# A decoder step on one core: value pages ahead of the last prompt sums, masked values on ScalarE, two roundings of the head outputs, keys transposed ahead of a split

## The chip, the cores and the metric

The kernel runs on one core of one Trainium2 chip. The metric is the device time of one execution in microseconds (us). TensorE (PE) multiplies matrices into PSUM, VectorE (DVE) and ScalarE (ACT) do the element-wise work, GpSimd (POOL) builds constants and issues the small loads and all of the state and cache outputs, and SyncE (SP) issues the large loads.

## What is computed

Two decoder layers, for 256 prompt tokens and for 8 decoding samples of 4 tokens each, 288 columns in all. A layer is a gated feed-forward block (FFN), a mixer, and a second FFN, each between a conditioned normalisation and a gated residual. The mixer runs three kinds of heads side by side and projects their outputs:

```
def mixer(a, w_in, w_out, ...):
    gq, gk, gv, gg, glr, mu, mv, sq, sk, sv = split_cols(a @ w_in)
    o_gla, s_gla = gla_mixer(gq, gk, gv, gg, glr, ..., gla_s0)      # 4 heads, recurrent state
    o_gm, v_gm = gmlp_mixer(mu, mv, ...)                            # 4 heads, spatial gating
    kk, vv = past keys and values (8 pages of 128 per sample), then the new ones
    o_sb = sb_attend(hs(sq), kk, vv, pos0, sb_b)                    # 8 heads, stick-breaking attention
    o = jnp.concatenate([o_gla, o_gm, o_sb], axis=-1) @ w_out
```

In the stick-breaking attention the weight of a key is exp(log_sigmoid(z) + a suffix sum of -softplus(z)). For the prompt this is a chain of matmuls with triangular matrices and element-wise steps for each of four head pairs; for the samples the keys and values come from pages of a cache in HBM.

## The kernel before

Activations lie transposed, features on the 128 partitions and the 288 columns in the free dimension. Every large matrix product is made of three fp32r products: weights and activations are split into a rounded part and a rest, `w_hi`, `w_lo` and `a_hi`, `a_lo`. For a weight step of 256 columns SP loads two halves of 512 KB into `raw` (two slots), ScalarE rounds each half into `w_hi` and VectorE makes `w_lo` (the helper `split`), and TensorE multiplies 48 times (16 output and input block pairs, three products each).

One loop body holds a layer, so each line below runs twice. The order of the work is written out by hand, engine by engine: every engine runs its own list in order and waits on semaphores. What stands behind a waiting instruction on the same engine waits too.

The mixer's input product has twelve weight steps (MI 0 to 11). After steps 3 to 10 TensorE multiplies two chunks of key pages each (`key_chunk`, 16 chunks of 4 pages, 1 MB each, in four slots of `direct`). VectorE transposes each chunk in place first (`turn_keys`, L1750). `KEYS_AT` gives the two chunks of a step. SP has the loads of key chunks 0 to 3 between those of steps 3 and 4. ScalarE's list has, in step 3, first the split of step 5, then the copy of the row bias (L1336), for which TensorE's sum of the means (L885) waits.

Then comes the stretch without weight steps, some 95 us in each layer. TensorE's list there mixes: the prompt pairs' scores, sums (`prompt_sums`, L933 and L934) and values (`prompt_values`, L944 and L946); the recurrent heads; the samples' value pages (`value_chunk(0..15)`, L830, 16 chunks through the same four slots of `direct`: chunk n is loaded once chunk n-4 has been used); `new_values` (L841), which closes a group of four samples; transposes of new key and value rows for the outputs (`rows_of`, L953); and the update of the samples' state, a product of `gvk` with `vm` (L1112), the value rows masked for each sample, which GpSimd makes (L2104) in the memory of slot 0 of `raw`.

When both groups of samples are done, ScalarE copies the sums out (`sample_rows`, L1424), TensorE transposes them (`turn_rows`, L849), ScalarE puts the heads in place in `Y` (`sample_heads`, L1435), and `Y` is rounded in four pairs of blocks, all 288 columns at a time, into `a_hi` (L1487) and `a_lo` (L1988). Then the output product runs its four steps (MO 0 to 3). Its first step is:

```
pe.wait_ge(lo_done.sem, lo_done.at(l, 2 * POS_MO + 2))
pe.wait_ge(yb_free.sem, yb_free.at(l, KB + 2 + 1))
last = paired_products(0, (0, 1), lambda k: pe.wait_ge(heads_ready.sem, heads_ready.at(l, k + 1)))
```

`yb_free` is raised by ScalarE at L1492, behind its split of MO step 1: `split(l, POS_MO, 0, 1)` and then `act.sem_inc(yb_free.sem, 2)`. The arrays `gvk`, `a_turn` and `a_keys` share memory with `w_hi`; `kst`, `o_rows` and `S` share memory with `w_lo`. So the splits of MO steps 0 and 1 wait for `outs_done`, which GpSimd raises when its output DMAs have landed.

## Time and profile before

| | us |
|---|---|
| median of 3 runs | 1523.11 |
| lowest, highest | 1519.5, 1530.31 |
| the profiled execution | 1520.16 |
| its span, first to last instruction | 1518.6 |
| TensorE busy | 1392.4 (92%) |
| VectorE busy | 822.9 (54%) |
| ScalarE busy | 589.5 (39%) |
| GpSimd busy | 56.5 (4%) |

The mean granted TensorE clock is 0.961 of full speed. The two layers repeat the same program: the mixer of the first lies at about 302 to 524 us of the span, that of the second at about 1036 to 1258 us.

### The profile page before, as it was taken

What the parts mean: (1) busy time and instruction counts of PE and PEld (TensorE: products, weight loads), DVE (VectorE), ACT (ScalarE), POOL (GpSimd) and SP (SyncE); (2) the same over time, 40 slices, a digit from 0 to 9 for tenths busy, and PEclk for the clock granted to TensorE, in tenths of its full rate; (3) what the DMA queues carried; (4) which work ended last, traced back from release to release, by engine and by line L of the source; (5) the groups of instructions that cost most, each with busy time, mean ns of one, the idle gap of its engine ahead of it and who ended that gap; (6) DMA issues with size and microseconds to landing.
All of it is one profiled execution on the core that took longest, in us unless ns stands there. A gap on an engine that the chain in (4) does not pass through costs nothing.

```text
span 1518.6 us, 36144 instructions
## 1 busy us (share of the span) xinstructions
PE 1392.4 (92%) x13844; PEld 1301.6 (86%) x13844; DVE 822.9 (54%) x1221; ACT 589.5 (39%) x949; POOL 56.5 (4%) x130
## 2 busy tenths in 40 slices
PE   5899999989886899999979999998997778999996
PEld 4899999789764889999969999987995577999996
DVE  2544544657972564554454455355789336455544
ACT  2423333523533543334453333354253345333344
POOL 3000000100110000000000000010002100000000
PEclk9899999999988999999989999999998979999998
DMA  9797597699757795555658858859994769765453
GB/s 313 244 279 220 158 303 219 189 295 292 243 198 239 238 319 160 163 149 150 181 161 278 256 160 253 261 171 282 273 301 163 254 179 322 209 165 166 142 164 113
DMA packets 432268, 335.16 MB, mean 221 GB/s; under 512 B 16087, under 2 KB 356343, under 8 KB 432128
## 3 DMA queue, kind: packets, MB, share of 16 engines
q1 hardware_dynamic: 429556, 327.52, 70.4%
q0 software_dynamic: 2272, 5.61, 1.1%
q8 instruction: 92, 1.51, 0.4%
q14 instruction: 48, 0.39, 0.1%
q10 hardware_dynamic: 300, 0.13, 0.0%
HBM read 328.41 MB, written 4.78 MB: 219 GB/s over the span
## 4 chain that ended last, share of the span: by engine, by line
PE 76%; DVE 7%; DMA 4%; SPq 4%; ACT 3%; issue 3%; DVEq 2%; ACTq 0%
PE PS L554 19%; PE PS L555 19%; PE PS L556 19%; PE PS L578 3%; PE PS L599 2%; PE PS L600 2%; PE PS L601 2%; PE PS L784 2%; SPq L460 2%; SPq L439 1%; PE PS L723 1%; PE PS L830 1%; PE PS L933 1%; DMA direct<-in_cache_sb_v 1%; DMA raw<-in_mix_w_in 1%
## 5 line engine op out<-in xcount | busy, mean ns | idle before, releaser
L1527 DVE TENSOR_TENSOR w_lo<-raw,w_hi 128x1024 fp32r<-128x1024 f32 (+1 forms) x371 | 396.1, 1106 | 530.7 <-ACT w_hi L1181 530.7
L1181 ACT ACTIVATE w_hi<-raw 128x1024 fp32r<-128x1024 f32 (+1 forms) x371 | 339.8, 960 | 726.1 <-PE PS L556 624.9
L554 PE MATMUL PS<-a_hi,w_hi 128*128 128x288 f32 x1664 | 497.9, 299 | 0.1
L555 PE MATMUL PS<-a_lo,w_hi 128*128 128x288 f32 x1664 | 490.9, 295 | 0.0
L556 PE MATMUL PS<-a_hi,w_lo 128*128 128x288 f32 x1664 | 489.3, 294 | 0.0
L554 PEld LDWEIGHTS PS<-a_hi,w_hi 128*128 128x128 f32 x1664 | 312.0, 188 | 8.2 <-issue 7.5
L556 PEld LDWEIGHTS PS<-a_hi,w_lo 128*128 128x128 f32 x1664 | 313.4, 188 | 0.0
L555 PEld LDWEIGHTS PS<-a_lo,w_hi 128*128 128x128 f32 x1664 | 312.4, 188 | 0.2
L554 PE MATMUL PS<-h_hi,w_hi 128*128 128x288 f32 x704 | 209.8, 298 | 0.0
L555 PE MATMUL PS<-h_lo,w_hi 128*128 128x288 f32 x704 | 209.1, 297 | 0.0
L556 PE MATMUL PS<-h_hi,w_lo 128*128 128x288 f32 x704 | 208.5, 296 | 0.0
L554 PEld LDWEIGHTS PS<-h_hi,w_hi 128*128 128x128 f32 x704 | 133.4, 189 | 2.2 <-issue 1.6
L555 PEld LDWEIGHTS PS<-h_lo,w_hi 128*128 128x128 f32 x704 | 132.1, 188 | 0.2
L556 PEld LDWEIGHTS PS<-h_hi,w_lo 128*128 128x128 f32 x704 | 132.1, 188 | 0.0
L599 PE MATMUL PS<-a_hi,w_hi 128*128 128x288 f32 x256 | 80.7, 315 | 28.3 <-DVE a_lo L1606 19.0
L578 PE MATMUL PS<-direct,cT 128*32 128x128 f32 x2560 | 87.5, 282 | 16.6 <-DMA direct<-in_cond_w 13.6
L578 PEld LDWEIGHTS PS<-direct,cT 128*32 128x32 f32 x2560 | 68.1, 112 | 31.9 <-issue 15.8
L599 PEld LDWEIGHTS PS<-a_hi,w_hi 128*128 128x128 f32 x256 | 51.2, 200 | 32.9 <-DVE a_lo L1606 18.5
L600 PE MATMUL PS<-a_lo,w_hi 128*128 128x288 f32 x256 | 78.6, 307 | 0.0
L601 PE MATMUL PS<-a_hi,w_lo 128*128 128x288 f32 x256 | 78.3, 306 | 0.0
L1750 DVE STREAM_TRANSPOSE direct<-direct 128x2048 f32<-128x2048 f32 x32 | 72.0, 2287 | 0.0
L830 PE MATMUL PS<-direct,a_keys 128*32 128x128 f32 x1024 | 37.0, 295 | 17.6 <-DMA direct<-in_cache_sb_v 13.0
(302 smaller groups left out, 1235.9 us busy)
## 6 DMA issues: line engine op xcount, KB each, us to landing
raw<-in_ffn_w_in SPq DMA_DIRECT2D x180, 512.0 KB, 4.8
direct<-in_cond_w SPq DMA_DIRECT2D x320, 256.0 KB, 4.9
direct<-in_cache_sb_k SPq DMA_DIRECT2D x128, 256.0 KB, 4.0
direct<-in_cache_sb_v SPq DMA_DIRECT2D x128, 256.0 KB, 3.8
...
raw<-in_mix_w_in SPq DMA_DIRECT2D x48, 512.0 KB, 6.9
...
raw<-in_mix_w_out SPq DMA_DIRECT2D x16, 512.0 KB, 6.0
```

The costliest lines, as they stand in the source:

```text
L460: sp.dma_start(direct[:, n % 4, 512 * t:512 * t + 512], src).then_inc(direct_in[n % 4].sem, 16)
L554: pe.matmul(out, whi, hi, start=begins and i == 0, stop=False)
L555: pe.matmul(out, whi, lo, start=False, stop=False)
L556: last = pe.matmul(out, wlo, hi, start=False, stop=ends and i == n - 1)
L578: last = pe.matmul(PS[32 * g:32 * g + 32, 6 + pair, 0:P], cT[:, 4 * half + kb, :], direct[:, slot, kb * 512 + g * P:kb * 512 + g * P + P], ...
L599: pe.matmul(out, whi, a_hi[:, k, :], start=k == 0, stop=False)
L600: pe.matmul(out, whi, a_lo[:, k, :], start=False, stop=False)
L601: last = pe.matmul(out, wlo, a_hi[:, k, :], start=False, stop=k == KB - 1)
L830: last = pe.matmul(PS[32 * p:32 * p + 32, 4, smp * P:smp * P + P], a_keys[:, 4 * half + t, 32 * p:32 * p + 32], direct[:, n % 4, 512 * t + ...
L1181: act.activation(w_hi[:, s, at_:at_ + n], raw[:, s, at_:at_ + n], ACT.Copy)\
L1527: tt(w_lo[:, s, at_:at_ + n], raw[:, s, at_:at_ + n], w_hi[:, s, at_:at_ + n], ALU.subtract).then_inc(lo_done.sem, 1)
L1750: dve.transpose(direct[:, n % 4, :], direct[:, n % 4, :]).then_inc(k_turned.sem, 1)
```

## The change

1. SP loads MI step 4's weights between key chunks 1 and 2; VectorE transposes key chunk 0 in step 2, ahead of its split of step 4, and no longer in step 3.
2. The prompt's and samples' key rows (`rows_of` with SK) are transposed and copied out at the start of the stretch, through bank 4 of PSUM, and no longer around the last prompt sums.
3. `vm` is made by ScalarE with 16 small activations, in slot 1 of `raw`, and no longer by GpSimd. SP loads MO step 0's weights ahead of value chunk 8 into slot 0, which is free for it, and the other steps behind chunk 15.
4. On TensorE value chunks 9, 10 and 11 come ahead of `prompt_sums(3)`, and both `prompt_values` ahead of chunk 14.
5. On ScalarE MO step 0 is split, and all but the samples' columns of blocks 4 to 7 is rounded, ahead of the last `sample_rows` and `sample_heads`; the 32 remaining columns of those four blocks are rounded by one more instruction on each of ScalarE and VectorE.
6. GpSimd's outputs change order, and the samples' state goes out last, behind `outs_done` and behind the last `new_values`.

```
--- before.py
+++ after.py
-        vm = [tile(f"vm{j}", [NS, B, P], F32, BASE + 4096 * j) for j in range(GP)]
+        vm = [tile(f"vm{j}", [NS, B, P], F32, BASE + 8192 + 4096 * j) for j in range(GP)]
...
-                key_chunks(l, 0, 1, 2, 3)
-                mix_in(4, 5)
+                key_chunks(l, 0, 1)
+                mix_in(4)
+                key_chunks(l, 2, 3)
+                mix_in(5)
...
                 for n in range(NPC):
+                    if n == 8:
+                        mix(l, mix_w_out, POS_MO, 0, 0, 0)
                     page_chunk(l, cache_sb_v, DP_V, 4 * n, n, n)
                 sp.wait_ge(ds_sum.sem, ds_sum.at(l, GP))
                 sp.sem_inc(raw_free.sem, 1)
-                for s in range(2):
-                    mix(l, mix_w_out, POS_MO, s, s, s * 256)
+                mix(l, mix_w_out, POS_MO, 1, 1, 256)
...
+                rows_of(0, SK, 4, k_t)
+                pe.wait_ge(kv_k.sem, kv_k.at(l, 1))
+                rows_of(1, SK, 4, k_t)
                 pe.wait_ge(gla_in.sem, gla_in.at(l, 1))
...
                 turn_new(0)
+                pe.wait_ge(kv_k.sem, kv_k.at(l, 2))
+                rows_of(2, SK, 4, k_t)
...
                 prompt_sums(2, 0)
+                value_chunk(9)
+                value_chunk(10)
+                value_chunk(11)
+                prompt_sums(3, 2)
                 pe.wait_ge(o_std.sem, o_std.at(l, 1))
-                rows_of(0, SK, 6, k_t)
-                rows_of(1, SK, 7, k_t)
-                value_chunk(9)
-                prompt_sums(3, 2)
...
-                value_chunk(10)
-                pe.wait_ge(o_headed.sem, o_headed.at(l, 1))
-                rows_of(2, SK, 5, k_t)
-                value_chunk(11)
                 value_chunk(12)
+                value_chunk(13)
                 pe.wait_ge(c_sub.sem, c_sub.at(l, 3))
                 prompt_values(0, 0)
-                value_chunk(13)
+                pe.wait_ge(c_sub.sem, c_sub.at(l, 4))
+                prompt_values(1, 2)
                 value_chunk(14)
                 value_chunk(15)
                 new_values(1)
-                pe.wait_ge(c_sub.sem, c_sub.at(l, 4))
-                prompt_values(1, 2)
-                pe.wait_ge(kv_k.sem, kv_k.at(l, 3))
+                pe.wait_ge(o_headed.sem, o_headed.at(l, 1))
                 turn_rows(1)
...
-                            heads_ready.sem, heads_ready.at(l, k + 1)))
+                            heads_ready.sem, heads_ready.at(l, k + 1 if k < 2 else KP + 1)))
...
+                def values_by_sample():
+                    for j in range(GP):
+                        for b in range(B):
+                            last = act.activation(vm[j][:, b, :], gvk[0:NS, 2, j * P:j * P + P], ACT.Copy,
+                                                  scale=same_s[:, b:b + 1])
+                        last.then_inc(vm_ready.sem, 1)
...
                 sample_weights(0)
+                key_rows(0, 4)
+                key_rows(1, 4)
                 prompt_scores(2)
...
                 weights_by_page(0)
+                key_rows(2, 4)
                 gla_rows(0, 6)
...
                 prompt_log1p_exp(1)
+                values_by_sample()
                 sample_weights(1)
...
                 act.wait_ge(outs_done.sem, outs_done.at(l, 1))
-                split(l, POS_MO, 0, 0, only=(0,))
-                sample_heads(1)
-                split(l, POS_MO, 0, 0, only=(1,))
-
-                act.drain()
+                act.wait_ge(ds_sum.sem, ds_sum.at(l, GP))
+                split(l, POS_MO, 0, 0)
                 act.wait_ge(gla_done.sem, gla_done.at(l, 1))
                 act.wait_ge(gm_done.sem, gm_done.at(l, 1))
+                act.wait_ge(op_sum.sem, op_sum.at(l, 2))
                 for k in range(KP):
                     if k >= 2:
                         act.wait_ge(op_evac.sem, op_evac.at(l, k - 1))
-                    act.activation(a_hi[:, 2 * k:2 * k + 2, :], Y[:, 2 * k:2 * k + 2, :], ACT.Copy)\
+                    n = T if k < 2 else NP
+                    act.activation(a_hi[:, 2 * k:2 * k + 2, 0:n], Y[:, 2 * k:2 * k + 2, 0:n], ACT.Copy)\
                         .then_inc(heads_round.sem, 1)
+                sample_rows(1)
+                sample_heads(1)
+                act.drain()
+                act.activation(a_hi[:, 4:8, NP:T], Y[:, 4:8, NP:T], ACT.Copy).then_inc(heads_round.sem, 1)
                 split(l, POS_MO, 0, 1)
...
                             .then_inc(q_rep.sem, 1)
+                        turn_keys(0)
...
                     for n in KEYS_AT.get(j, ()):
-                        turn_keys(n)
+                        if n:
+                            turn_keys(n)
```

VectorE in input step 2 and 3: `qrep` is the copy that ends step 2's first part, `w_lo` of 1024 columns a half of a weight split, `direct` a chunk of key pages. Before:

```order
L1805 COPY qrep<-Fm 128x512 [waits mix_evac]
L1526 REGISTER_ALU
L1527 TENSOR_TENSOR w_lo<-raw,w_hi 128x1024 [waits hi_done]
L1526 REGISTER_ALU
L1527 TENSOR_TENSOR w_lo<-raw,w_hi 128x1024 [waits hi_done]
L1809 STREAM_TRANSPOSE qt<-PS 128x512 [waits q_t]
L1744 TENSOR_TENSOR qb<-qt,row_part 128x512
L1749 ISA
L1750 STREAM_TRANSPOSE direct<-direct 128x2048 [waits direct_in0]
L1750 STREAM_TRANSPOSE direct<-direct 128x2048 [waits direct_in1]
```

The same place after the change:

```order
L1818 COPY qrep<-Fm 128x512 [waits mix_evac]
L1762 ISA
L1763 STREAM_TRANSPOSE direct<-direct 128x2048 [waits direct_in0]
L1539 REGISTER_ALU
L1540 TENSOR_TENSOR w_lo<-raw,w_hi 128x1024 [waits hi_done]
L1539 REGISTER_ALU
L1540 TENSOR_TENSOR w_lo<-raw,w_hi 128x1024 [waits hi_done]
L1823 STREAM_TRANSPOSE qt<-PS 128x512 [waits q_t]
L1757 TENSOR_TENSOR qb<-qt,row_part 128x512
L1763 STREAM_TRANSPOSE direct<-direct 128x2048 [waits direct_in1]
```

The transpose of chunk 0 stands ahead of the split of step 4, that of chunk 1 where it was.

ScalarE at the end of the stretch: `o_rows` and `Y` are `sample_rows(1)` and `sample_heads(1)`, `raw_in00` and `raw_in01` the two halves of MO step 0, `raw_in10` and `raw_in11` those of MO step 1. Before:

```order
L1405 ACTIVATE zp<-zp 128x768 [waits c_sub]
L1424 ACTIVATE o_rows<-PS 128x512 [waits o_rows_sum]
L1177 ISA [waits outs_done]
L1181 ACTIVATE w_hi<-raw 128x1024 [waits w_used,raw_in00]
L1435 ACTIVATE Y<-PS 64x4x4 [waits o_turned]
L1435 ACTIVATE Y<-PS 64x4x4 x7
L1181 ACTIVATE w_hi<-raw 128x1024 [waits raw_in01]
L1487 ACTIVATE a_hi<-Y 128x576 [waits gm_done,gla_done]
L1487 ACTIVATE a_hi<-Y 128x576
L1487 ACTIVATE a_hi<-Y 128x576 [waits op_evac] x2
L1181 ACTIVATE w_hi<-raw 128x1024 [waits w_used,raw_in10]
L1181 ACTIVATE w_hi<-raw 128x1024 [waits raw_in11]
```

The same place after:

```order
L1180 ISA [waits ds_sum,outs_done]
L1184 ACTIVATE w_hi<-raw 128x1024 [waits w_used,raw_in00]
L1184 ACTIVATE w_hi<-raw 128x1024 [waits raw_in01]
L1496 ACTIVATE a_hi<-Y 128x576 [waits op_sum,gm_done,gla_done]
L1496 ACTIVATE a_hi<-Y 128x576
L1496 ACTIVATE a_hi<-Y 128x2x256 [waits op_evac] x2
L1434 ACTIVATE o_rows<-PS 128x512 [waits o_rows_sum]
L1445 ACTIVATE Y<-PS 64x4x4 [waits o_turned]
L1445 ACTIVATE Y<-PS 64x4x4 x7
L1501 ACTIVATE a_hi<-Y 128x4x32
L1184 ACTIVATE w_hi<-raw 128x1024 [waits w_used,raw_in10]
L1184 ACTIVATE w_hi<-raw 128x1024 [waits raw_in11]
```

The split of step 0 and four roundings moved ahead of the samples' copies; one small rounding is left behind them, and the split of step 1, behind which `yb_free` is raised, stayed last.

TensorE from value chunk 9 on: `direct` with `a_keys` is a value chunk (16 rows of it stand as one and x15), `zp` with `sv` are `prompt_values`, `sn` with `suffix` the sums of pair 3. Before:

```order
L953 MATMUL PS<-ident,Fm 128x128 [waits o_std]
L953 MATMUL PS<-ident,Fm 128x128 x7
L830 MATMUL PS<-direct,a_keys 32x128 [waits direct_in1]
L830 MATMUL PS<-direct,a_keys 32x128 x15
L933 MATMUL PS<-sn,suffix 128x384 [waits sp_ready]
```

After:

```order
L833 MATMUL PS<-direct,a_keys 32x128 [waits direct_in1]
L833 MATMUL PS<-direct,a_keys 32x128 x15
L833 MATMUL PS<-direct,a_keys 32x128 [waits direct_in2]
L833 MATMUL PS<-direct,a_keys 32x128 x15
L833 MATMUL PS<-direct,a_keys 32x128 [waits direct_in3]
L833 MATMUL PS<-direct,a_keys 32x128 x15
L936 MATMUL PS<-sn,suffix 128x384 [waits sp_ready]
```

The eight key transposes are gone from there, and two more value chunks stand ahead of the sums.

## Rows read from the trace of the kernel before
**Rows 1.** timeline of PE, input steps 3, 4: start, us, line [idle before]
```profile
329.52 1.93 PE L784 MATMUL PS<-direct,qb 128*32 128x128 f32 x32 [4.75 <-DVE direct L1750]
...
335.25 0.64 PE L554 MATMUL PS<-a_hi,w_hi 128*128 128x288 f32 x1
```

**Rows 2.** timeline of ACT in the same place
```profile
323.53 1.06 ACT L1181 ACTIVATE w_hi<-raw 128x1024 fp32r<-128x1024 f32 x1 [0.59 <-DMA raw<-in_mix_w_in]
...
327.34 1.06 ACT L1181 ACTIVATE w_hi<-raw 128x1024 fp32r<-128x1024 f32 x1 [0.34 <-DMA raw<-in_mix_w_in]
328.30 0.15 ACT L1336 ACTIVATE row_bias<-PS 128x1 f32<-128x1 f32 x1
```

**Rows 3.** timeline of SP, the issues of one chunk of pages
```profile
458.29 2.03 SPq L460 DMA_DIRECT2D direct<-in_cache_sb_v  x4
```

**Rows 4.** timeline of POOL in the stretch
```profile
425.10 3.76 POOL L2104 TENSOR_TENSOR vm<-gvk,same_s 32x1024 f32<-32x1024 f32 x2 [11.22 <-ACT gvk L1410]
...
454.09 1.16 POOL L2116 DMA_DIRECT2D out<-sv  x2 [17.79 <-ACT sv L1415]
```

**Rows 5.** timeline of DVE, two instructions for either sample group
```profile
404.14 0.20 DVE L1773 COPY totals<-sm 128x32 f32<-128x32 f32 x1
...
404.32 1.24 DVE L1775 TENSOR_TENSOR z<-z,sm 128x1040 f32<-128x1040 f32 x1
...
425.20 1.83 DVE L1773 COPY totals<-sm 128x32 f32<-128x32 f32 x1
...
427.02 2.94 DVE L1775 TENSOR_TENSOR z<-z,sm 128x1040 f32<-128x1040 f32 x1
```

**Rows 6.** timeline of PE in the middle
```profile
432.50 1.09 PE L1038 MATMUL PS<-wst,vn 128*64 128x128 f32 x16 [2.55 <-DVE att_s L1914]
434.53 0.64 PE L1045 MATMUL PS<-wss,vn 32*64 32x32 f32 x8 [0.93 <-DVE wss L1929]
```

**Rows 7.** stretches: us, busy PE, PEld, DVE, ACT, POOL, clock, DMA, GB/s
```profile
434.50:441.70 7.20, 7.17 (x56) 5.39 (x56) 5.05 (x7) 1.16 (x2) 1.23 (x2) 0.53 0.58 207
...
461.89:478.89 17.00, 12.95 (x238) 8.95 (x236) 4.84 (x6) 4.71 (x7) 3.41 (x5) 1.00 0.66 214
...
496.26:504.25 7.99, 7.99 (x50) 7.99 (x51) 4.13 (x5) 1.79 (x2) 0.00 (x0) 0.81 0.81 220
504.25:510.70 6.45, 6.45 (x51) 6.45 (x50) 2.36 (x2) 3.22 (x5) 0.00 (x0) 1.00 0.42 116
```

**Rows 8.** timeline of ACT at the stretch's start
```profile
416.31 0.62 ACT L1391 ACTIVATE zp<-PS,sb 128x128 f32<-128x128 f32 x2 [3.10 <-DVE zp L1857]
```

**Rows 9.** timeline of PE in the tail
```profile
461.89 1.04 PE L953 MATMUL PS<-ident,Fm 128*128 128x128 f32 x8
...
484.02 1.94 PE L830 MATMUL PS<-direct,a_keys 128*32 128x128 f32 x32 [5.13 <-DMA direct<-in_cache_sb_v]
...
487.75 1.13 PE L944 MATMUL PS<-zp,sv 128*64 128x256 f32 x4
...
490.56 1.12 PE L849 MATMUL PS<-ident,o_rows 128*128 128x128 f32 x4
496.26 0.58 PE L599 MATMUL PS<-a_hi,w_hi 128*128 128x288 f32 x1 [4.58 <-DVE a_lo L1988]
```

**Rows 10.** timeline of ACT in the tail
```profile
462.53 1.09 ACT L1420 ACTIVATE kst<-PS 128x512 f32<-128x512 f32 x2 [2.08 <-PE PS L953]
...
491.71 0.80 ACT L1435 ACTIVATE Y<-PS 64x16 f32<-64x16 f32 x8 [2.29 <-PE PS L849]
```

**Rows 11.** DMA, median us to landing: value chunk 12, MO step 0
```profile
direct<-in_cache_sb_v SPq DMA_DIRECT2D x4, 256.0 KB, 3.8
...
raw<-in_mix_w_out SPq DMA_DIRECT2D x2, 512.0 KB, 8.7
```

**Rows 12.** chain that ended last, 430 to 515 us: chunk 15
```profile
476.25 7.72 DMA direct<-in_cache_sb_v
```

**Rows 13.** list of waits, 300 to 515 us: total, times, longest
```profile
PEld PS L599 <- ACTq L1492: 5.0, 1, 5.0
```

53 lines of the change are left out of this document (24 added, 29 removed).

## The prediction

> **What bounds the kernel now.** TensorE is busy for 1392.4 of 1518.6 us (the table above), so I read where it is not busy, first in the list of waits and then in its timeline with ScalarE's and VectorE's beside it. What this change can reach lies in the two mixers, in six gaps per layer. I work them out in the first layer; the second repeats them. Times are of the profiled execution (1520.16 us), which lies 3.0 us under the median of 1523.11.
>
> **Input steps 3 and 4.** TensorE ends step 3 at about 324.8, then idles 4.75 us until VectorE has transposed key chunk 0 (329.52), and starts step 4 at 335.25 [rows 1]. The chain behind it: the second half of step 4's weights lands at 323.5, the second half of step 5's at 327.3 [rows 2], VectorE splits step 4, turns the queries, and only then transposes two chunks. After the change step 4's weights are asked for two chunks earlier. A chunk's four issues take 2.03 us and a look at the page table before them about 0.6 [rows 3], so the weights land 5.3 us earlier, at 318.2, about when slot 0 of `w_hi` is free again. VectorE transposes chunk 0 while it would idle, has split step 4 by 321, the queries by 322.2 and chunk 1 by 324.5. So TensorE takes chunk 0 at once. From 329.52 to 335.25 the two chunks and the mean take 5.73 us at the lower clock; at the full one half, 2.9. That gives 327.7, but the mean waits for the row bias, which stands in ScalarE's list behind the split of step 5. That weight has the same bytes ahead of it as before, so I take the same landing: bias at 328.4 [rows 2], mean 1.1 us, step 4 at 329.6. **Gain 5.7 us**; 7.5 if step 5's weights land 2 us sooner; 4 if VectorE's chunk 1 slips by 1.5. Behind it the steps are full again: TensorE has some 9 us of work per step, VectorE 7.5, so the shift is kept.
>
> **The middle.** GpSimd makes `vm` from 425.10 for 3.76 us [rows 4]. Just then VectorE's copy of 32 columns takes 1.83 us and its subtraction 2.94; the same two took 0.20 and 1.24 at 404 [rows 5]. With `vm` on ScalarE these 3.3 us go. TensorE waits behind exactly this VectorE chain: 2.55 us at L1038 and 0.93 at L1045 [rows 6], 3.5 us, of which the third key row copy (0.6 on ScalarE, ahead of `gvk`) takes back 0.5: 3.0. Then the clock: from 434.5 to 441.7 TensorE was busy all the time at a granted clock of 0.53, near its lower level of 1.2 GHz [rows 7], right behind these two idle times. About 6.2 of the 7.2 us ran at half speed; at 2.4 GHz they are 3.1, so the clock gives 3.0 if it stays up, 0 if not. Without the two idle times TensorE works on without a break, so I take it. **Gain 6.0**, 2.5 to 6.5.
>
> `vm` itself is 16 activations of 128 columns. The nearest row is a pair of 128 columns with a bias pointer, 0.62 [rows 8], 0.31 each, 5.0 us for 16; the eight of 16 columns in 0.80 [rows 10] bound it below, 1.6. They begin at about 429.9, behind the second prompt exponential, and ScalarE next waits for VectorE's offsets, due near 434; 5.0 us ends at 434.9, and VectorE comes to the result only at about 436.5. So it is hidden; at over 0.4 each it would show.
> The Trainium skill, "ScalarE: Activation LUTs", section "What ACT_TABLE_LOAD costs", gives 186 ns + 0.833 ns per element, 93 ns more for a pointer operand and 93 ns of overlap: an estimate of 0.29 us each here, 4.7 us together; the row's 0.31 is close, and no row shows this form itself.
> The first two key copies stand on ScalarE where it idles 3.10 us for VectorE [rows 8]; with two hops to TensorE they take about 2.6, so the prompt scores behind them start when they did.
> The Trainium skill, "SBUF — State Buffer", section "Who interferes with whom", says that GpSimd and VectorE lock a shared port pair for whole instructions and the later one fully blocks. The trace agrees so far: the slow copy ends where the first half of GpSimd's work does, 427.0. By the rule all 3.3 us go; without it none would, the middle would bring 0, and the time would be 1474.
>
> **The tail.** From 461.89 (key rows, now gone from here) to 478.89 TensorE was busy 12.95 us at full clock [rows 7]: chunks 9 to 14, the last sums, the `vm` product, the first `prompt_values`. Take off the key rows, 1.04 for two and half of it for the third [rows 9]: 11.4. Add chunk 15 and `new_values` (3.73 at the lower clock from 484.02 on, 2.0 at the full one) and the second `prompt_values` (2.81 from 487.75 on, 1.5 at the full one) [rows 9]: 14.9. If nothing is waited for it ends at 476.8. What could be late:
> - The sums of pair 3. ScalarE copied two key rows ahead of the exponential, with 2.08 idle and 1.09 busy [rows 10]; without them its part ends 3.1 us earlier, VectorE's at 464.0, and TensorE arrives at 465.0.
> - Pair 3's weights. TensorE now has chunks 14, 15 and `new_values` queued behind them. Sums end at 466.9, `vm` at 468.8, then VectorE's two state additions and its step to 470.4, ScalarE to 471.3. TensorE arrives at 472.3.
> - Chunk 15. It is asked for when chunk 11 has been used (465.0) and two chunks stand ahead on SP, 2.65 us each: issued by 470.5, landing 3.8 later [rows 11], at 474.3. TensorE arrives at 474.8. Half a microsecond of room, the tightest point.
> - MO step 0's split: its weights landed at 441, the last rows that `outs_done` stands for are asked for at 454 [rows 4] and should land by 462, both before 471.3, when ScalarE is free. Then split (2.0), VectorE's part, and the rounding of four pairs end at 478.6.
>
> From 476.8: `o_rows` copy 0.65, transposes 0.6 (1.12 at the lower clock, [rows 9]), `sample_heads` 0.8 [rows 10], rounding and issue 0.6, in all 479.5; the first step can't start under them, since `yb_free` is raised behind them and behind step 1's split. The list of waits shows that very gate before [rows 13]. It needs step 1's weights, issued at 471, landed by 477 to 479. I take 479.8 against 496.26 [rows 9]: 16.5. MO step 0 ran at 0.81 of the clock for 7.99 us, the next in 6.45 [rows 7]; half of that difference, 0.8. **Gain 17.3**, 12 to 18.
>
> **Sum.** 5.7 + 6.0 + 17.3 = 29.0 a layer, 58 for both: 1520.2 - 58 = 1462. Part of the 3 us to the median added, **1463**. With all lower ends, 4 + 2.5 + 12 = 18.5 a layer, 1483; with the upper ones 32, 1456.
>
> **Rivals.**
> A. *Landings take the gap's place.* The last chunk landed 7.7 us after its issue, and the first output weights 8.7 [rows 11, 12]. If that came again, chunk 15 would land at 477.9, 3.1 late, and step 1's weights, behind it, would hold `yb_free`: 3.5 us a layer, 1470. For it: these very transfers. Against it: then kst and the state went out at the same time, and they no longer do.
> B. *The clock stays low in the middle and falls again before MO*, since shorter idle times ahead of both places remain: 3.8 a layer, 1470.
> C. *The front doesn't do what it says*: step 5's weights or the reordered DMAs land as late as step 4's did, TensorE's wait only moves to the mean: gain 0 to 1, 1472.
> D. *Two or three of these at once*: 1480 to 1492.
> E. *Slower than before*, one mechanism: ScalarE now waits for `outs_done` at 471, ahead of all rounding and of `sample_rows(1)`; before it waited at 488. GpSimd raises it after key, value and prompt state rows have landed. Each us beyond about 474 costs one. The value rows are asked for at 454 [rows 4]; even at the slowest landing above, 8.7, they are there at 464. The stall would have to last 29 us, to 503, for the kernel to lose; it would then give 1523 or more.
>
> **Chances.** Forecast 0.5; A 0.15; B 0.13; C 0.08; D 0.08; nothing gained net 0.03; E 0.03. A measurement of this kernel can tell about 1% (15 us) from no change. All cases but the last two are faster by more: faster 0.94, same 0.03, slower 0.03. The range takes in the forecast with its bounds and A to C, and the lower half of D: 1453 to 1485.
>
> **What would show it.** Step 4 starts some 5 us after step 3's end (10.5 before), with the bias copy just ahead of the mean. L1775's counterpart takes 1.24 in all four places. The clock in the middle is 1.00. Chunk 15 is waited for under 1 us. From `new_values` to MO step 0 it is under 4 us, and the last releaser is ScalarE. I would be wrong if TensorE waited over 2 us for pages or for pair 3's weights, or if MO step 0 waited for `raw`.

## The result, and the profile after

The changed kernel takes 1470.54 us in the median of four runs (1469.78 to 1474.85), the kernel before 1525.09 in the four beside it. The ratio is 0.9674, 95% interval 0.9649 to 0.9699: faster by 3.3%. Timed a second time it took 1467.54 beside 1521.13, ratio 0.9667 (0.9637 to 0.9696). The prediction was 1463, range 1453 to 1485.

The first profiled execution (1474.85 us) is the slowest of the four; a second profile of the same kernel (1464.45 us) is used further down. The head of its page, with the shares of the chain:

```profile
span 1473.3 us, 36182 instructions
PE 1382.7 (94%) x13844; PEld 1298.5 (88%) x13844; DVE 815.7 (55%) x1223; ACT 598.9 (41%) x983; POOL 49.2 (3%) x126
PE 81%; DVE 4%; DMA 4%; SPq 4%; ACT 3%; issue 2%; DVEq 1%; ACTq 0%
```

TensorE's work is the same 13844 products; what went is idle time and time at the low clock. Times below are of the first layer's mixer unless another is named, and line numbers are 3 higher up to about L1000. A row of a timeline gives the start, the length, engine, line, operation and tiles, and in brackets how long the engine idled before it and what ended that wait.

**Input steps 3 and 4** [rows 1, 2]. VectorE's timeline, then TensorE's, then ScalarE's:

```profile
319.33 2.30 DVE L1763 STREAM_TRANSPOSE direct<-direct 128x2048 f32<-128x2048 f32 x1
...
326.79 2.30 DVE L1763 STREAM_TRANSPOSE direct<-direct 128x2048 f32<-128x2048 f32 x1
```

```profile
329.26 1.96 PE L787 MATMUL PS<-direct,qb 128*32 128x128 f32 x64
331.55 1.23 PE L888 MATMUL PS<-Fm,ones 128*128 128x288 f32 x4 [0.34 <-ACT row_bias L1339]
332.41 0.51 PE L557 MATMUL PS<-a_hi,w_hi 128*128 128x288 f32 x1
```

```profile
329.36 2.00 ACT L1184 ACTIVATE w_hi<-raw 128x1024 fp32r<-128x1024 f32 x2 [4.79 <-PE PS L559]
331.28 0.15 ACT L1339 ACTIVATE row_bias<-PS 128x1 f32<-128x1 f32 x1
```

Chunks 0 and 1 run as 64 products in one piece at the full clock, with no wait, where there had been 4.75 us. The mean waits 0.34 for the row bias, and step 4 starts 3.1 us after the end of step 3, against 10.5.

**The middle** [rows 4 to 7]. VectorE's copy and subtraction, ScalarE's `vm`, TensorE behind them, and windows of 4 or 8 us (length, then the busy us and instructions of PE, PEld, DVE, ACT and POOL, then the granted clock, the DMA share and GB/s):

```profile
421.49 0.19 DVE L1786 COPY totals<-sm 128x32 f32<-128x32 f32 x1
...
421.66 1.23 DVE L1788 TENSOR_TENSOR z<-z,sm 128x1040 f32<-128x1040 f32 x1
```

```profile
426.00 1.09 PE L1046 MATMUL PS<-wst,vn 128*64 128x128 f32 x16
427.47 0.42 PE L1053 MATMUL PS<-wss,vn 32*64 32x32 f32 x8 [0.38 <-DVE wss L1944]
```

```profile
424.00:432.00 8.00, 7.62 (x158) 6.00 (x149) 7.59 (x19) 7.27 (x20) 1.22 (x2) 1.00 0.95 329
432.00:440.00 8.00, 8.00 (x185) 6.81 (x185) 4.32 (x7) 0.81 (x2) 0.00 (x0) 1.00 1.08 340
...
468.00:472.00 4.00, 2.10 (x13) 0.92 (x6) 0.49 (x2) 1.78 (x11) 1.82 (x2) 0.50 1.05 288
472.00:480.00 8.00, 8.00 (x51) 8.00 (x52) 2.59 (x3) 1.99 (x3) 0.00 (x0) 0.83 0.63 172
```

The idle 2.55 and 0.93 us are 0 and 0.38, and the granted clock is 1.00 where it was 0.53. ScalarE's 16 activations for `vm` take 4.77 us (the row is shown with the run of the kernel before that has them), 0.30 each. ScalarE's next instruction starts at 430.18, and VectorE's result that it needs is there at 430.15, so they delay it by next to nothing.

**The tail** [rows 9 to 13]. TensorE from the last sums on:

```profile
454.88 0.91 PE L936 MATMUL PS<-sn,suffix 128*128 128x384 f32 x2
...
460.72 0.66 PE L947 MATMUL PS<-zp,sv 128*64 128x256 f32 x4
...
466.38 1.08 PE L833 MATMUL PS<-direct,a_keys 128*32 128x128 f32 x32 [1.78 <-DMA direct<-in_cache_sb_v]
467.40 1.42 PE L844 MATMUL PS<-sv,a_new 32*32 32x512 f32 x8
469.60 1.08 PE L852 MATMUL PS<-ident,o_rows 128*128 128x128 f32 x4 [0.79 <-ACT o_rows L1434]
471.80 0.61 PE L602 MATMUL PS<-a_hi,w_hi 128*128 128x288 f32 x1 [1.11 <-ACTq L1505]
```

Neither the sums of pair 3 nor its weights are waited for. Chunk 15 is, 1.78 us (2.61 in the second layer). MO step 0 starts 24.98 us behind value chunk 8, against 39.29 before. Its last releaser is ScalarE's queue at L1505, the flag `yb_free`. The flag stands behind the split of step 1 but doesn't wait for its end: that split runs from 471.81 to 473.80, and the step starts at 471.80. Its products take 0.24 us each, the lower clock; the windows above show 0.50 and then 0.83.

**Where the rest of the gain was.** From step 3's end to MO step 0 the two mixers are shorter by 29.0 and 26.4 us, but the span by only 45.3. The missing 10.1 us lie in the three stretches outside, which the change doesn't touch: 4.6, 2.5 and 3.1. TensorE waits for the condition weights there for 17.3 us instead of 13.6; most of the rest is that the same products took longer (301.1 us instead of 296.7 ahead of the first mixer's step 3, granted clock 0.97 instead of 0.98). Ahead of the first mixer the weights were issued in 8.70 us, against 7.43 in the trace before:

```profile
295.57 1.08 PE L581 MATMUL PS<-direct,cT 128*32 128x128 f32 x32 [1.65 <-DMA direct<-in_cond_w]
298.26 1.94 PE L581 MATMUL PS<-direct,cT 128*32 128x128 f32 x32 [1.61 <-DMA direct<-in_cond_w]
300.12 0.61 PE L602 MATMUL PS<-a_hi,w_hi 128*128 128x288 f32 x1
```

The mixer starts 2.8 us late and at the lower clock. Were that chance alone, the change would be worth 55, which is the difference of the two medians (54.6). But a late start also changes what the mixer's front costs, so the two must be taken together.

To do that I cut each mixer in every trace at marks that no edit touches: **A** from TensorE's first sum of squares ahead of the mixer (L723; L726) to the mean (L885; L888), **B** from there to value chunk 8, **C** from there to the first product of MO step 0. The two numbers of a cell are the two layers, in us.

| kernel | median | ratio (95%) | A | B | C | B + C |
|---|---|---|---|---|---|---|
| before | 1525.09 | | 47.8 48.0 | 123.4 123.2 | 39.3 39.5 | 162.7 162.7 |
| changed | 1470.54 | 0.9674 (0.9649 to 0.9699) | 46.1 44.8 | 115.3 117.1 | 25.0 25.4 | 140.3 142.4 |
| changed, again | 1467.54 | 0.9667 (0.9637 to 0.9696) | 43.5 43.0 | 119.2 118.5 | 21.9 21.6 | 141.1 140.1 |
| vm on GpSimd | 1474.94 | 0.9695 (0.9664 to 0.9725) | 42.8 42.9 | 118.6 118.4 | 22.2 21.8 | 140.8 140.2 |
| front undone | 1475.28 | 0.9688 (0.9659 to 0.9717) | 46.8 47.3 | 117.1 116.8 | 22.5 24.6 | 139.6 141.4 |
| MO weights early | 1468.08 | 0.9639 (0.9614 to 0.9664) | 44.6 42.8 | 116.0 119.4 | 22.3 25.1 | 138.3 144.5 |
| flag ahead of heads | 1464.16 | 0.9623 (0.9598 to 0.9648) | 43.3 43.0 | 116.7 116.8 | 21.4 20.3 | 138.1 137.2 |
| before, vm on ScalarE | 1513.85 | 0.9945 (0.9919 to 0.9972) | 48.2 48.0 | 118.1 118.6 | 41.3 41.3 | 159.3 159.9 |
| PE order undone | 1490.02 | 0.9795 (0.9767 to 0.9823) | 45.7 43.5 | 117.2 117.1 | 33.2 33.1 | 150.4 150.2 |
| rounding whole | 1474.59 | 0.9686 (0.9657 to 0.9714) | 45.8 43.6 | 115.1 115.7 | 25.7 24.1 | 140.8 139.8 |
| pair 0 under heads | 1464.01 | 0.9628 (0.9596 to 0.9660) | 42.8 43.2 | 115.1 118.0 | 22.5 21.9 | 137.6 139.9 |
| values order undone | 1480.31 | 0.9738 (0.9715 to 0.9760) | 43.3 42.8 | 117.6 118.3 | 27.6 27.4 | 145.2 145.8 |
| chunk 9 ahead of sums 2 | 1458.56 | 0.9586 (0.9564 to 0.9608) | 43.2 43.4 | 117.3 118.0 | 21.7 21.9 | 139.1 139.9 |

Half an interval is some 4 us, so a time alone tells less than that from nothing; the columns tell more. B and C vary by 4 us against each other in one and the same kernel: a long B is followed by a short C. Between the two profiles of the changed kernel C differs by 3.5 us on the mean, of which 1.3 are waits for pages and 2.2 are time that TensorE is busy, at the lower clock. So B + C is what I compare. C ends with the first product of MO step 0; what the clock costs in that step lies behind it.

### The profile page after: what moved, and what is told of

Read it like the earlier page. It is cut to its first block, busy times and chain, and to the rows that moved or that the text cites. A ratio compares the mean times of both kernels' runs of the same rounds, so it can differ in the third digit from the quotient of the medians.

```text
span 1473.3 us, 36182 instructions
## 1 busy us (share of the span) xinstructions
PE 1382.7 (94%) x13844; PEld 1298.5 (88%) x13844; DVE 815.7 (55%) x1223; ACT 598.9 (41%) x983; POOL 49.2 (3%) x126
## 4 chain that ended last, share of the span: by engine, by line
PE 81%; DVE 4%; DMA 4%; SPq 4%; ACT 3%; issue 2%; DVEq 1%; ACTq 0%
PE PS L557 21%; PE PS L558 20%; PE PS L559 20%; PE PS L581 4%; PE PS L602 3%; PE PS L603 3%; PE PS L604 3%; SPq L439 2%; DMA direct<-in_cond_w 2%; PE PS L787 1%; PE PS L833 1%; PE PS L726 1%; DMA direct<-in_cache_sb_v 1%; SPq L460 1%; PE PS L936 1%
## 5 line engine op out<-in xcount | busy, mean ns | idle before, releaser
L558 PEld LDWEIGHTS PS<-a_lo,w_hi 128*128 128x128 f32 x1664 | 312.5, 188 | 0.2
L581 PE MATMUL PS<-direct,cT 128*32 128x128 f32 x2560 | 90.2, 288 | 20.0 <-DMA direct<-in_cond_w 17.3
L603 PEld LDWEIGHTS PS<-a_lo,w_hi 128*128 128x128 f32 x256 | 53.1, 207 | 0.0
```

The costliest lines, as they stand in the source:

```text
L558: pe.matmul(out, whi, lo, start=False, stop=False)
L581: last = pe.matmul(PS[32 * g:32 * g + 32, 6 + pair, 0:P], cT[:, 4 * half + kb, :], direct[:, slot, kb * 512 + g * P:kb * 512 + g * P + P], ...
L603: pe.matmul(out, whi, a_lo[:, k, :], start=False, stop=False)
```

## The experiments

### vm on GpSimd again

```
 POOL, behind the key rows' issues:
+                after(gvk_a, l, 2)
+                pool.tensor_tensor(out=vm[j], in0=gvk[...], in1=same_s[...], op=ALU.mult)   (j = 0, 1)
 ACT:
-                values_by_sample()
```

> The changed kernel with one part undone: GpSimd makes vm again (two products of 32x1024, in slot 1 of raw, between its issues of the key rows and of the prompt state), ScalarE no longer does. Median of the changed kernel: 1470.5. My theory: the middle's gain of 7.2 us (layer 1) and 6.2 us (layer 2) comes from this alone. VectorE's copy of 32 columns and its subtraction beside GpSimd take about 1.8 and 2.9 us instead of 0.19 and 1.23; TensorE idles 2.5 to 3.5 us at the wst and wss products, and the granted clock falls to about 0.5 behind them, so value chunk 8 comes 5 to 7 us later in each layer. In the tail some of it is given back, because chunk 15, which TensorE waits 1.8 and 2.6 us for, does not come later by as much: 4 to 6 a layer remain, 1478.5 to 1482.5. The Trainium skill, 'SBUF — State Buffer', section 'Who interferes with whom', says that GpSimd and VectorE lock a shared port pair; by it the long VectorE instructions come back. Rival 1: the middle's gain came from the key rows that were moved and from the tail's shift, and vm's engine makes no difference: 1469 to 1472. Rival 2: the stall comes back but not the clock: 2 to 3 a layer, 1475 to 1476.5.

Measured: ratio 0.9695, 4 us above the changed kernel's first median, 7 above its second, by the ratios 3 to 4, inside the uncertainty; B + C 140.8 and 140.2 against 140.1 to 142.4. **The theory's price fell.** GpSimd's and VectorE's timelines in this kernel:

```profile
420.18 5.48 POOL L2133 TENSOR_TENSOR vm<-gvk,same_s 32x1024 f32<-32x1024 f32 x2 [0.42 <-ACT gvk L1413]
```

```profile
420.11 1.23 DVE L1787 TENSOR_TENSOR z<-z,sm 128x1040 f32<-128x1040 f32 x1
421.42 2.49 DVE L1886 SCALAR_TENSOR_TENSOR sn<-zp,sn 128x768 f32<-128x768 f32 x1
```

Before, GpSimd began 0.10 us ahead of VectorE's copy; it ran undisturbed in 3.76 and VectorE lost 3.3 [rows 4, 5]. Here VectorE's subtraction began 0.07 us ahead; it takes its 1.23, GpSimd is stretched to 5.48, and only the next VectorE instruction is long (2.49, 0.96 before). The second layer repeats it (1127.58 and 1127.59, 2.49, 5.54). So the two do shut each other out, and which starts first settles who waits first. VectorE lost 1.5, and TensorE waited for none of it: VectorE's part was done at 425.36, and TensorE came to L1046 at 426.95. It had run chunks 0 and 1 at the lower clock (3.52 us for 64 products, 1.95 at the full one), but 1.6 us earlier it would have found VectorE's part just done as well. So in the changed kernel B is 4.8 us shorter than before with `vm` on GpSimd as well; which edit moved GpSimd's start behind VectorE's no run shows.
The Trainium skill, "SBUF — State Buffer", section "Who interferes with whom", has whoever issues first lock the shared port pair for the whole instruction, while the other fully blocks; both traces agree with it.

### The kernel before with vm on ScalarE

```
 POOL:
-                pool.tensor_tensor(out=vm[j], ...)   (j = 0, 1)
 ACT:
                 prompt_log1p_exp(1)
+                values_by_sample()
                 sample_weights(1)
```

> The kernel before with one part of the change alone: ScalarE makes vm with its 16 activations, behind the second prompt exponential, in the place in memory that it had. The last run undid the same part in the changed kernel and gave an unclear answer: GpSimd began 1.4 us behind value chunk 0's start there and 1.8 us in the kernel before, VectorE's copy and subtraction were done first, and only one VectorE instruction was stretched (2.49 us instead of 0.96), GpSimd's two taking 5.48 instead of 3.76. Theory: the price depends on which instruction comes first; in the kernel before it was GpSimd's both times (3.3 us), and TensorE's 2.55 and 0.93 and the clock at 0.5 come from it. Then from value chunk 0 to chunk 8 the kernel before needs 29 us instead of 33.7, and its tail, which waits for chunks that are asked for when others are used, moves with it: 4 to 5 us a layer, 1512 to 1515 beside 1522 to 1525. Rival 1: the waits for pages in the tail (1.7 to 5.1 us) grow by what the middle gains: 1519 to 1525. Rival 2: vm's engine doesn't matter and the middle's gain is that of the key rows: no VectorE instruction there changes and the time stays.

VectorE's, then ScalarE's, then TensorE's timeline, with one window:

```profile
425.21 0.19 DVE L1781 COPY totals<-sm 128x32 f32<-128x32 f32 x1
...
425.39 1.23 DVE L1783 TENSOR_TENSOR z<-z,sm 128x1040 f32<-128x1040 f32 x1
```

```profile
431.31 4.77 ACT L1425 ACTIVATE vm<-gvk,same_s 32x128 f32<-32x128 f32 x16
```

```profile
462.41 3.68 PE L1112 MATMUL PS<-vm,gvk 32*64 32x512 f32 x8
...
481.59 1.93 PE L830 MATMUL PS<-direct,a_keys 128*32 128x128 f32 x32 [5.76 <-DMA direct<-in_cache_sb_v]
```

```profile
460.00:466.00 6.00, 6.00 (x16) 2.24 (x16) 0.69 (x1) 0.00 (x0) 0.00 (x0) 0.60 0.42 136
```

Measured: ratio 0.9945, 8.4 us by the ratio, 7.4 by the medians. Alone, in the place where GpSimd had come first, the part brings what the mechanism promises: both VectorE instructions are short, TensorE's 2.55 and 0.93 us are gone, the granted clock is 1.00 from 428 to 444, and B is 5.0 us shorter. In C 1.9 us of it are lost again, from 39.4 to 41.3, but not as rival 1 had it: from chunk 9 on TensorE waits 5.95 and 6.20 us for pages, against 6.82 and 6.17 before. What grew is the low clock. The `vm` product takes 3.68 us, where it took 1.93 before, the clock granted around it is 0.60, and chunk 11 is used 18.5 us behind chunk 8 instead of 15.8. It stays 3.1 us a layer in B + C. The forecast, 1512 to 1515, held.

### The front undone

```
 SP:
-                key_chunks(l, 0, 1)
-                mix_in(4)
-                key_chunks(l, 2, 3)
-                mix_in(5)
+                key_chunks(l, 0, 1, 2, 3)
+                mix_in(4, 5)
 DVE: turn_keys(0) in step 3 again, not in step 2
```

> The changed kernel with the front undone: step 4's weights are asked for behind key chunk 3 again and key chunk 0 is transposed in step 3. My theory: step 3's end to step 4's start goes from 3.4 us back to about 10.5 us, TensorE's wait of 4.75 us for key chunk 0 returns, and all of it reaches the end: 6.2 to 7.2 a layer, 1483 to 1485. Rival: the steps behind have slack (VectorE has 7.5 us of work in a step of 9), so part of the shift is caught up before the middle, or the middle waits for VectorE anyway: under 3 a layer, 1471 to 1476.5.

Measured: 1475.28, 5 to 8 us above the changed kernel by the medians, 2 to 3 by the ratios, inside the uncertainty, and not 13. My price of 6.2 to 7.2 a layer was wrong. A says why. With the old front it is 47.7 on the mean of six mixers (46.8 to 48.2), with the new one 43.7 of twenty (42.8 to 46.1): 4.0 a layer. I had measured from step 3. But the first profile's mixers started late, and their weights were there when TensorE came, so the mean waited only 0.34 us; where the mixer starts on time the mean waits for the row bias. TensorE's and ScalarE's timelines in the second layer of the changed kernel's second profile:

```profile
1036.52 1.69 PE L888 MATMUL PS<-Fm,ones 128*128 128x288 f32 x4 [2.31 <-ACT row_bias L1339]
```

```profile
1033.56 1.06 ACT L1184 ACTIVATE w_hi<-raw 128x1024 fp32r<-128x1024 f32 x1 [5.98 <-DMA raw<-in_mix_w_in]
1035.28 1.06 ACT L1184 ACTIVATE w_hi<-raw 128x1024 fp32r<-128x1024 f32 x1 [0.66 <-DMA raw<-in_mix_w_in]
1036.24 0.15 ACT L1339 ACTIVATE row_bias<-PS 128x1 f32<-128x1 f32 x1
```

Step 5's weights are then the last to land, and the row bias stands behind their split. With the old front a late start was hidden: in this kernel the first mixer's products begin 14.6 us after the first sum of squares and the second's 11.3, and the wait for key chunk 0 is 1.07 and 4.90 us, so step 4 starts after 47.7 and 48.2. With the new front it isn't: step 4 starts after 44.0 us in the thirteen mixers that began on time (11.1 to 12.1) and after 45.7 in the seven late ones.

### MO step 0's weights ahead of chunk 4

```
                 for n in range(NPC):
-                    if n == 8:
+                    if n == 4:
                         mix(l, mix_w_out, POS_MO, 0, 0, 0)
```

> The changed kernel, but SP asks for the weights of MO step 0 ahead of value chunk 4 instead of ahead of value chunk 8. What it tests: why chunk 15 came 1.78 us (layer 1) and 2.61 us (layer 2) late, where I had forecast under 1. My theory: from 420 to 472 us the DMA share is 0.9 to 1.1 in every window of 4 us, so bytes and not the freeing of slots set when chunk 15 lands; these weights (1 MB, about 3 us at 350 GB/s) take part in that stretch, while from 404 to 420 the share is 0.03 to 0.37. Loaded there, they free 3 us: the wait for chunk 15 goes to 0 to 0.3, 2 us a layer, 1466 to 1467; if the clock then stays up until the handoff, up to 1.5 more a layer, 1463. Rival: chunk 15's landing is set by the use of chunk 11 and a fixed latency of its own: the wait stays at 1.5 to 2.6 and the time at 1469 to 1472.

Measured: 1468.08, and chunk 15 waited for 1.59 and 2.44 us. The rival held: moving 1 MB out of the stretch left the wait, and from the end of chunk 11 to chunk 15 it took 11.6 and 11.9 us, against 11.4, 12.1, 10.7 and 10.3 in the changed kernel's four mixers. So the count starts at the slot. In the changed kernel's first profile TensorE ends chunk 11 at 454.9, SP's four issues for chunk 15 run from 458.89 to 460.92, behind those of 13 and 14, and the pages are there at 466.4.

### The flag ahead of the heads

```
+                act.sem_inc(yb_free.sem, 2)
                 sample_rows(1)
                 sample_heads(1)
                 act.drain()
                 act.activation(a_hi[:, 4:8, NP:T], ...)
                 split(l, POS_MO, 0, 1)
-                act.sem_inc(yb_free.sem, 2)
```

> The changed kernel, but ScalarE raises yb_free (banks 0 to 3 of PSUM are free) right behind the rounding of the four pairs, ahead of the last sample_rows and sample_heads, instead of behind its split of MO step 1. My theory: TensorE's last idle time, 1.11 us before MO step 0, is for this flag alone, since the first two pairs are rounded in full by 468.4. It goes; pairs 0 and 1 take 24 products, 5.8 us at the lower clock, so the 32 late columns (ready at 472.3) aren't waited for. 1.1 us a layer, 1468 to 1469. The clock stays low in MO step 0, since chunk 15's wait and the 0.79 us for o_rows remain ahead of it. Rival: the step then waits for the late columns or for w_lo instead and nothing is gained, 1470 to 1471; or the clock comes up earlier, 3 us a layer, 1464 to 1465.

Measured: 1464.16, ratio 0.9623: 3 to 6 us under the changed kernel's medians; its interval overlaps that of the second timing. The idle time of 1.11 us before MO step 0 is gone, and in this profile, the fastest of the five runs (1456.21), the clock stayed up as well, the second rival. TensorE's timeline and two windows:

```profile
467.69 0.63 PE L852 MATMUL PS<-ident,o_rows 128*128 128x128 f32 x4 [0.81 <-ACT o_rows L1434]
468.07 0.38 PE L602 MATMUL PS<-a_hi,w_hi 128*128 128x288 f32 x1
468.29 0.29 PE L603 MATMUL PS<-a_lo,w_hi 128*128 128x288 f32 x1
```

```profile
468.00:472.00 4.00, 4.00 (x33) 4.00 (x32) 1.77 (x3) 2.99 (x11) 1.51 (x2) 1.00 1.03 284
472.00:480.00 8.00, 8.00 (x63) 8.00 (x62) 3.24 (x3) 3.20 (x4) 0.00 (x0) 1.00 0.54 146
```

A product every 0.13 us from the first on. From MO step 0's start to the next product with the condition weights it takes 28.25 us in both layers, against 29.6 to 31.1 in the changed kernel. Chunk 15 was 0.66 and 0.81 us late here, so less idle time lay ahead; how much of the clock the flag itself kept up, one profile can't say.

### TensorE's order undone, whole and in half

The whole, shortened (the second kernel has only its last edit, `prompt_values(1, 2)` behind `new_values(1)`):

```
-                value_chunk(9); value_chunk(10); value_chunk(11); prompt_sums(3, 2)
+                value_chunk(9); prompt_sums(3, 2)
                 vm products
-                value_chunk(12); value_chunk(13); prompt_values(0, 0)
-                prompt_values(1, 2); value_chunk(14); value_chunk(15); new_values(1)
+                value_chunk(10); value_chunk(11); value_chunk(12); prompt_values(0, 0)
+                value_chunk(13); value_chunk(14); value_chunk(15); new_values(1)
+                prompt_values(1, 2)
```

> The changed kernel with TensorE's order in the tail undone: value chunk 9, prompt_sums(3), the vm product, chunks 10 to 12, the first prompt_values, chunks 13 to 15, new_values, the second prompt_values. Theory: both things that the order was forecast to bring are lost. prompt_sums(3) comes 2 us earlier than its VectorE and ScalarE part (ready at about 454.5 us in the changed kernel's trace) and waits 0 to 1 us, and ScalarE, which waits for both prompt_values before it rounds, does four roundings (2.4 us) and only then o_rows and the heads, behind new_values and not ahead of it. MO step 0 starts 3 to 4 us later in each layer: 1476 to 1478. Rival: the tail is bound by how fast pages come (DMA share 1.0 from 444 to 472), chunk 15's wait takes the difference, and only the roundings show or nothing does: 1469 to 1473.

> The changed kernel with one half of TensorE's new order undone: the second prompt_values stands behind new_values again, chunks 9 to 11 stay ahead of prompt_sums(3). Undoing both halves cost 19.5 us, where I had expected 6 to 7. Theory: most of it is this half, because ScalarE waits for both prompt_values before it rounds anything, so all four roundings and only then the copy of o_rows follow on TensorE's last product: from chunk 15 to MO step 0 there were 12.0 us instead of 5.4, 6.6 a layer. Then this kernel needs 6 to 6.6 us a layer more than the changed one less the 1.4 us by which TensorE is earlier at chunk 15 if the page is there: 1480 to 1483. The rest, 3 us a layer, would be chunks 9 to 11 behind prompt_sums(3): their slots come free later, and chunk 15 lands 3.7 us later. Rival: the halves are worth the other way round, the pages 7 and the roundings 3: 1475 to 1477.

Measured: 1490.02 and 1480.31; B + C is 9.3 us longer with both halves undone and 4.5 with one, on the means. My first forecast of 3 to 4 a layer was far too small. TensorE's timeline of the whole:

```profile
465.58 1.08 PE L833 MATMUL PS<-direct,a_keys 128*32 128x128 f32 x32 [1.49 <-DMA direct<-in_cache_sb_v]
470.13 1.94 PE L833 MATMUL PS<-direct,a_keys 128*32 128x128 f32 x32 [3.48 <-DMA direct<-in_cache_sb_v]
...
479.92 1.09 PE L852 MATMUL PS<-ident,o_rows 128*128 128x128 f32 x4 [3.18 <-ACT o_rows L1434]
482.12 0.61 PE L602 MATMUL PS<-a_hi,w_hi 128*128 128x288 f32 x1 [1.11 <-ACTq L1505]
```

and ScalarE's where only the values are moved:

```profile
468.36 2.30 ACT L1496 ACTIVATE a_hi<-Y 128x576 fp32r<-128x576 f32 x4 [4.94 <-PE PS L949]
470.68 0.60 ACT L1434 ACTIVATE o_rows<-PS 128x512 f32<-128x512 f32 x1
```

The second forecast, made with the first result, held in the time (1480 to 1483 against 1480.31), not in its parts: it gave the values 6 to 6.6 a layer and the pages 3. By the medians (1467.54 beside it) the values are worth 6.4, by B + C of the profile, the fastest of its five runs, 4.5. There four roundings and then `o_rows` follow TensorE's last product. The other 4.8 in B + C are the pages: with chunks 10 and 11 behind the sums and the `vm` product their slots come free nearly 6 us later, and chunk 15 lands at 470.1 instead of 466.4.

### The rounding in one part

```
+                sample_rows(1); sample_heads(1); act.drain()
                 for k in range(KP):
                     if k >= 2: act.wait_ge(op_evac.sem, ...)
-                    n = T if k < 2 else NP
-                    act.activation(a_hi[:, 2*k:2*k+2, 0:n], ...)
+                    act.activation(a_hi[:, 2*k:2*k+2, :], ...)
-                sample_rows(1); sample_heads(1); act.drain()
-                act.activation(a_hi[:, 4:8, NP:T], ...)
 (VectorE's part and TensorE's wait for the fifth rounding likewise)
```

> The changed kernel with the rounding in one part: ScalarE copies the samples' sums and puts their heads in place first, and then rounds all 288 columns of the four pairs; VectorE likewise. TensorE's order stays. Theory: between the last heads and MO step 0 stand one rounding of 0.6 and its VectorE part of 0.7 more for the first pair, and the flag yb_free comes behind all four, so MO step 0 starts 2.4 to 3.3 us later than in the changed kernel: 5 to 6.5 us in all, 1475.5 to 1477. Rival: MO step 0 is bound by its weights or by what TensorE does last, and the rounding is hidden: 1469 to 1472.

Measured: 1474.59, ratio 0.9686; B + C 140.8 and 139.8, inside the changed kernel's spread. The step that I looked for is there, but smaller. TensorE's timeline:

```profile
468.78 1.09 PE L852 MATMUL PS<-ident,o_rows 128*128 128x128 f32 x4 [0.81 <-ACT o_rows L1434]
472.45 0.58 PE L602 MATMUL PS<-a_hi,w_hi 128*128 128x288 f32 x1 [2.59 <-DVE a_lo L2000]
```

2.59 us instead of 1.11: only the first pair's rounding and its VectorE part are on the path, since TensorE starts on pair 0 while the others are rounded. I had counted all four, since the flag stands behind them; but it was up when MO step 0 started, at 472.45, and ScalarE rounded until 473.23. 1.5 a layer is below what this comparison can show in the time.

### Two versions that go further

Pair 0 under the heads, on top of the flag ahead and the early weights:

```
-                pe.wait_ge(o_headed.sem, o_headed.at(l, 1))
-                turn_rows(1)
 MO step 0, called for each pair of blocks:
+                def pair_ready(k):
+                    if k == 1:
+                        pe.wait_ge(o_headed.sem, o_headed.at(l, 1))
+                        turn_rows(1)
+                    pe.wait_ge(heads_ready.sem, heads_ready.at(l, k + 1 if k < 2 else KP + 1))
```

> The changed kernel with three edits to its end: MO step 0's weights ahead of chunk 4, yb_free raised ahead of the last sample_rows, and on TensorE the products of pair 0 of MO step 0 directly behind new_values, with the transposes of the last rows between pair 0 and pair 1. The flag alone gave 1464.2 (1456.2 in the profiled run), the weights alone 1468.1 with chunk 15 still 1.6 and 2.4 us late, so these weights weren't what made it late. Theory: TensorE's idle 0.8 us for o_rows goes as well, pair 0 (12 products, 1.6 us at full clock) hides o_rows, pair 1 hides half of the heads; new_values to the end of MO step 0 gets shorter by 1.9 to 2.5 a layer against the changed kernel, and by 0.8 against the flag alone: 1462 to 1464. With less idle time the clock at MO step 0, 0.5 for some 3 to 6 us now, may stay up: then up to 3 us a layer more, 1457 to 1460. Rival: the step then waits for the late columns (pairs 2 and 3) for as long as it started earlier: 1464 to 1467.

Measured: 1464.01, the same as the flag alone. MO step 0 does start 1.2 and 1.6 us behind the start of `new_values`, instead of 2.3 with the flag alone, but chunk 15 was 2.63 and 2.39 us late, and the clock was low in step 0 (0.50 from 465.9 to 470.0): nothing net.

The last version keeps pair 0 under the heads, has the weights ahead of chunk 8 again, and changes what TensorE does when ScalarE's `a_keys` isn't ready:

```
+                turn_rows(0)
                 value_chunk(8)
-                turn_rows(0)
+                value_chunk(9)
                 prompt_sums(2, 0)
-                value_chunk(9)
                 value_chunk(10)
                 value_chunk(11)
```

> The version with the flag ahead of the heads and pair 0 of MO step 0 ahead of the last transposes, MO step 0's weights ahead of chunk 8 as in the changed kernel, and on TensorE the transposes of the first group's rows ahead of chunk 8 and chunk 9 ahead of prompt_sums(2). Theory: what still bounds the tail is how early the slots of chunks 8 to 11 come free, since chunk 15 lands some 11.5 us after chunk 11's use. TensorE waits 2.3 us at chunk 8 for ScalarE's a_keys; the transposes (0.6) fill a part of it, and chunk 9's slot comes free 2 us earlier, chunks 10 and 11 as before. Chunk 15 comes 0.5 to 1.5 us earlier: 1461 to 1463. Rival: chunk 9 itself has not landed then (it was waited for 1.6 us in one profile), TensorE waits for it instead of doing the sums, and the time is 1464 to 1467.

> The changed kernel itself, unaltered, as the mark for the kernels timed with it, and as a second profile of the mixers. Theory: the two mixers differ from run to run by what comes ahead of them. In the first profile the first products of both mixers started 14.7 and 14.5 us after the squares of the normalisation (condition weights late by 2 to 3 us), in six of the eight other profiled mixers with 11.1 to 12.7; where that start was late, the mean in step 3 did not wait, and where it was early the mean waited 1.4 to 2.6 us for the row bias. So the sum from the squares to the mean is 42.8 to 46.1 with the new front and 46.8 to 48.2 with the old one. I expect 42.8 to 46 again, and a median of 1468 to 1472. Rival: the first runs were on a slow stretch of the chip or a quick one, and the median is off by more than 4 us.

Measured beside each other: 1458.56 for this version, under its forecast of 1461 to 1463, and 1467.54 for the changed kernel again, half a microsecond under its own; the ratios are 0.9586 (0.9564 to 0.9608) and 0.9667 (0.9637 to 0.9696), whose intervals don't touch. It beats both kernels. TensorE's timeline:

```profile
445.81 1.95 PE L833 MATMUL PS<-direct,a_keys 128*32 128x128 f32 x64 [1.29 <-ACT a_keys L1335]
...
450.54 1.08 PE L833 MATMUL PS<-direct,a_keys 128*32 128x128 f32 x32 [0.85 <-DMA direct<-in_cache_sb_v]
453.23 1.56 PE L833 MATMUL PS<-direct,a_keys 128*32 128x128 f32 x32 [1.61 <-DMA direct<-in_cache_sb_v]
...
464.36 1.95 PE L833 MATMUL PS<-direct,a_keys 128*32 128x128 f32 x64
467.53 0.37 PE L602 MATMUL PS<-a_hi,w_hi 128*128 128x288 f32 x1 [0.23 <-DVE a_lo L2007]
```

Chunks 14 and 15 run in one piece here; in the second layer chunk 15 is waited for 2.83 us. Its profiled execution (1464.53) is its slowest, so the traces don't show where its typical run gains 9 us. They show the waits for pages moved ahead in the first layer, but not shorter in sum (2.46 and 2.83 us). And it differs from the changed kernel in three edits: the flag, pair 0 and TensorE's order. No run has the last alone, and its interval overlaps that of the version before (0.9596 to 0.9660).

No run undoes the move of the key rows, the loading and splitting of MO step 0 ahead of the last heads, or GpSimd's order; what these are worth by themselves is open.

## Why the prediction was right, and where it was off

**The front** was forecast at 5.7 (4 to 7.5). The steps came true: chunk 0 taken at once, full clock, the bias copy just ahead of the mean as the last gate. The landing of step 5's weights, kept at 327.3, was right as well: the rounding of their second half starts 41.1 and 41.5 us after the first sum of squares before, 41.7 and 42.3 in the changed kernel's second profile. So was the wait for it: in mixers whose first products start within 12.2 us of the first sum of squares the mean waits 1.4 to 2.9 us; by the prediction's numbers TensorE would have been there at 326.7 and the bias at 328.4, 1.7 us. Up to the start of step 4, where the forecast ends, the thirteen mixers that start on time gain 5.5 us on the kernel before and its `vm` version (A ends at the start of the mean and misses its full clock). What the forecast left out is the late start, which the old front hid: the seven late mixers gain 3.8, and three of the changed kernel's four are among them.

**The middle** was forecast at 6.0 (2.5 to 6.5). B is shorter by 3.9 to 8.3 us, 6.2 on the mean of eighteen mixers, 0.8 of it the mean itself, which the forecast has at the front. The mechanism is shown in the kernel before: GpSimd's `vm` stretched VectorE's two instructions, TensorE waited and the clock fell; with `vm` on ScalarE alone B is 5.0 shorter. The step "by the rule all 3.3 us go" held there. What I didn't see is that this price hangs on which engine starts first by 0.1 us: in the changed kernel, with `vm` back on GpSimd, B keeps 4.8 of the gain. So that `vm`'s engine brought the middle's gain in the changed kernel isn't shown. Nor did I see that a shorter B is partly paid back in C.

**vm on ScalarE**: 5.0 us forecast, 4.77 measured; hidden, as forecast. The estimate from the Trainium skill ("ScalarE: Activation LUTs", section "What ACT_TABLE_LOAD costs") was 4.7, and the trace agrees with it.

**The tail** was forecast at 17.3 (12 to 18). C is shorter by 14.3 and 14.1 in the first profile, 17.4 and 17.9 in the second. Pair 3's sums and weights were not waited for, and from `new_values` to MO step 0 it took 3.0 us behind its end, as worked out (476.8 to 479.8). Two terms were off. Chunk 15, "half a microsecond of room", was 0.8 to 2.6 us late: I had 5.5 us from the use of chunk 11 to the last issue and 3.8 to the landing, and it took 6.0 and 5.4. The 5.5 came near by luck: it counts two chunks of 2.65 and no time for chunk 15's own issues, and chunk 13 had all but been issued when chunk 11 was used (455.1 and 454.9). The landing of 3.8 was the row of chunk 12 before; here chunk 15 stood behind two other chunks just asked for, at a DMA share of 1.0. One of my signs of being wrong, over 2 us of waiting for pages, came in one of the four mixers (2.61). And the 0.8 us for a better clock in MO step 0 did not come: the step took 7.8 to 9.3 us, 7.99 before; in the profile with the flag ahead it took 6.45.

**The sum** was 29.0 a layer. Against the mark ahead of the mixer the four mixers of the two profiles give 25.3 (210.5 less 185.3), 50.6 in all; the medians give 54.6 and 53.6. So 3 to 7 us of the 58 did not come. By the means of the four, cut at the start of step 4, the front gave 4.3, the middle 5.1 and the tail 15.9, against 5.7, 6.0 and, up to MO step 0, 16.5; the last 0.8 is the clock in that step.

**The rivals.** A, landings in the gap's place, came true in half its size (chunk 15), not by the output weights. B held for the clock ahead of MO, not for the middle. C, D and E did not; ScalarE was never held by `outs_done`.
